# Stick-breaking attention: value products issued right ahead of the scores, and ScalarE's work in another order

## The reference

```
q, k, v, gate = split(h @ w_in, 4)          # q, k get an RMS norm per head
z = q . k / sqrt(64)                        # for keys before the query
log1m = -softplus(z)                        # 0 where masked
after = sum of log1m over the keys between this one and the query
wts = exp(log_sigmoid(z) + after)           # 0 where masked
o = wts @ v;   y = (o * silu(gate)) @ w_out
```

## Time and profile before

| what | value |
| --- | --- |
| median of 3 runs | 1758.52 us (1758.38 to 1759.03) |
| the profiled execution's own time | 1758.74 us |
| its span, first to last instruction | 1756.9 us |
| TensorE busy | 1741.8 us, 99% of the span |
| VectorE, ScalarE, GpSimd busy | 887.9, 826.3, 654.1 us |
| the attention layer's steps, first scores to last value products | 568.5 to 761.6 us of the span |

### The profile page before, as it was taken

The page is one execution under the profiler, slowest core; times in us unless marked ns, Lnnn a source line. Parts: engine busy times, 40 slices in busy tenths (PEclk is TensorE's granted clock), DMA queues, the critical chain, the costliest instruction groups (busy, mean ns, idle before and its releaser), DMA issues.

```text
span 1756.9 us, 22619 instructions
## 1 busy us (share of the span) xinstructions
PE 1741.8 (99%) x8786; PEld 1418.8 (81%) x8786; DVE 887.9 (51%) x1329; ACT 826.3 (47%) x1191; POOL 654.1 (37%) x238
## 2 busy tenths in 40 slices
PE   8999999999999999999999999999999999999999
PEld 6688899888898666678888888888877888998887
DVE  6765964453133777745734433341287568435500
ACT  5575343785233776744422222222266734348720
POOL 1333420344434655444244444444324234114442
PEclk9999999999999999999999999999999999999999
DMA  4223210222222111122222222222222232012222
GB/s 177 89 80 97 73 43 8 95 96 96 96 96 73 49 49 49 49 72 96 86 106 95 95 95 95 95 95 96 84 96 72 73 118 64 13 49 96 96 96 72
DMA packets 48776, 143.70 MB, mean 82 GB/s; under 512 B 28080, under 2 KB 30256, under 8 KB 32816
## 3 DMA queue, kind: packets, MB, share of 16 engines
q1 hardware_dynamic: 48688, 142.50, 23.9%
HBM read 137.25 MB, written 5.24 MB: 81 GB/s over the span
## 4 chain that ended last, share of the span: by engine, by line
PE 88%; DVE 6%; ACT 4%; issue 1%; DMA 0%; POOL 0%; SPq 0%; ACTq 0%; DVEq 0%
PE ps L1662 22%; PE ps L1664 22%; PE ps L1663 22%; PE ps L1928 3%; DVE acc L1154 2%; PE ps L1989 2%; PE ps L1955 2%; PE ps L2118 1%; PE ps L1975 1%; PE ps L1939 1%; PE ps L1984 1%; PE ps L2164 1%; DVE acc L1157 1%; PE ps L2062 1%; PE ps L2064 1%
## 5 line engine op out<-in xcount | busy, mean ns | idle before, releaser
L467 POOL TENSOR_TENSOR w_lo<-w_raw,w_hi 128x2048 fp32r<-128x2048 f32 x105 | 496.6, 4730 | 805.2 <-ACT w_hi L598 802.1
L1662 PE MATMUL ps<-h_hi,w_hi 128*128 128x512 f32 x1488 | 594.1, 399 | 4.2 <-DVE h_lo L1027 2.1
L1664 PE MATMUL ps<-h_hi,w_lo 128*128 128x512 f32 x1488 | 580.4, 390 | 0.0
L1663 PE MATMUL ps<-h_lo,w_hi 128*128 128x512 f32 x1488 | 579.5, 389 | 0.0
L1662 PEld LDWEIGHTS ps<-h_hi,w_hi 128*128 128x128 f32 x1488 | 279.4, 188 | 83.1 <-issue 21.1
L1664 PEld LDWEIGHTS ps<-h_hi,w_lo 128*128 128x128 f32 x1488 | 279.2, 188 | 59.8
L1663 PEld LDWEIGHTS ps<-h_lo,w_hi 128*128 128x128 f32 x1488 | 279.6, 188 | 55.9 <-issue 1.4
L598 ACT ACTIVATE w_hi<-w_raw 128x2048 fp32r<-128x2048 f32 (+1 forms) x126 | 238.7, 1895 | 129.4 <-PE ps L1664 123.8
L1662 PE MATMUL ps<-y_hi,w_hi 128*128 128x512 f32 x448 | 174.3, 389 | 0.0
L1663 PE MATMUL ps<-y_lo,w_hi 128*128 128x512 f32 x448 | 174.3, 389 | 0.0
L1664 PE MATMUL ps<-y_hi,w_lo 128*128 128x512 f32 x448 | 174.3, 389 | 0.0
(11 more groups left out here) (211 smaller groups left out, 2332.2 us busy)
## 6 DMA issues: line engine op xcount, KB each, us to landing
w_raw<-w_tiles SPq DMA_DIRECT2D x124, 1024.0 KB, 4.9
x<-x_t SPq DMA_DIRECT2D x4, 512.0 KB, 7.0
out_t<-x SPq DMA_DIRECT2D x8, 256.0 KB, 5.7
w_raw<-w_tiles SPq DMA_DIRECT2D x2, 512.0 KB, 5.0
scr_u<-lt SPq DMA_DIRECT2D x8, 128.0 KB, 2.7
u_blk<-scr_u SPq DMA_DIRECT2D x2, 512.0 KB, 3.3
scr_t<-v_t SPq DMA_DIRECT2D x2, 512.0 KB, 2.6
scr_v<-v_blk SPq DMA_DIRECT2D x2, 512.0 KB, 3.3
```

The costliest lines, as they stand in the source:

```text
L467: pool.tensor_tensor(w_lo[:, slot, :], w_raw[:, slot, :], w_hi[:, slot, :].bitcast(F32), ALU.subtract).then_inc(lo_done, 1)
L1662: pe.matmul(out_, w_h, m_h, start=start, stop=False)
L1663: pe.matmul(out_, w_h, m_l, start=False, stop=False)
L1664: return pe.matmul(out_, w_l, m_h, start=False, stop=stop)
```

## The change

Three orders are changed; no instruction is added, removed or resized.

- On TensorE, pv(g-2) goes from behind the blocks to the head of the step, right before z(g). The blocks that stood around it are now two before cum(g-1) and two after (in the last pair one and one).
- On ScalarE, in v = 2 and v = 3 weights(g-1) goes from behind softplus(g) to a place inside it, between Exp and Ln. In v = 0 and v = 1 it stays behind.
- On ScalarE, `hi` of tile t0 + 7 + j goes from the end of v = 2 in pair j to v = 0 of pair j + 1, behind softplus and before square_qk. The last one (pair 7, v = 3) stays.

```diff
@@ ScalarE, softplus(g, between)
                 for e in range(2):
                     act.wait_ge(b["abs"], 2 * g + e + 1)
                     act.activation(sb_t[:, e, 0:w], sb_t[:, e, 0:w], ACT.Exp, scale=-1.0).then_inc(b["exp"], 1)
+                if g % 4 > 1:
+                    weights(g - 1)
                 for e in range(2):
                     act.wait_ge(b["exp"], 2 * g + e + 1)
                     act.activation(sb_t[:, e, 0:w], sb_t[:, e, 0:w], ACT.Ln, bias=1.0).then_inc(b["ln1"], 1)
@@ ScalarE, the loop over pairs and steps
                     softplus(g, j + 1 if more and v == 3 else None)
+                    if v == 0 and j:
+                        hi(t0 + 6 + j)
                     if more and v == 0:
                         square_qk(j + 1, 0)
                     if more and v == 1:
                         rms_qk(j + 1, 0)
-                    if g:
+                    if g and v < 2:
                         weights(g - 1)
-                    if v == (2 if more else 3):
+                    if v == 3 and not more:
                         hi(t0 + 7 + j)
@@ TensorE, the loop over pairs and steps
                     g = 4 * j + v
+                    if g >= 2:
+                        pv(g - 2)
                     z(g)
                     if more and v == 3:
                         sums(j + 1, 1)
                     fill(2 if more else 1)
                     if more and v == 1:
                         sums(j + 1, 0)
-                    if g >= 2:
-                        pv(g - 2)
-                    fill(1 if more else 0)
                     if g:
                         cum(g - 1)
-                    fill(1)
+                    fill(2 if more else 1)
```

## The result

The changed kernel takes 1762.13 us (median of 13 runs, 1761.28 to 1763.62); the kernel before took 1758.96 us in the 13 runs beside it. The ratio is 1.0018 with a 95% interval of 1.001 to 1.0026: slower, by 3.2 us. The forecast was 1763.1 us, range 1757 to 1767.5, slower with a chance of 0.60. The profiled execution took 1762.0 us with a span of 1760.2.

What follows compares the result with a forecast made beforehand. TensorE, busy 99% of the span, was taken as the bound. Gains of 6.0 and 1.5 us against losses of 9.6 and 2.5 us gave +4.6 us on 1758.52: 1763.1 us, range 1757 to 1767.5.

Steps and rivals of the forecast that it cites:

- The join: TensorE, value products (pv) put right before scores (z): about 0.20 us saved per step, 30 places, 6.0 us.
- The chain on ScalarE: From z(v3)'s start: softplus sum at 5.90 us, z(v0) at 6.55, ScalarE's weights letting pv(v3) start at 13.27.
- The wait in v = 0: TensorE waits ahead of pv(v3) for ScalarE's weights: 1.6 us in each of six pairs, 9.6 us; last pair 2.5.
- my sum: TensorE's timeline from z(v3)'s start without the new wait: z(v0) at 6.55 us, ready for pv(v3) at 11.68.
- the last pair's other steps: Last pair outside v0: less time for ScalarE but an old wait gone; nothing was taken for these.
- Where the wait stands: The whole new wait, some 1.6 us per pair, was placed ahead of pv(v3), at the head of v = 1.
- TensorE stays the bound: Rival: weights(v3) ready by 11.68 us, so only gains count: 7.5 us less, 1751.0 us; chance 0.12.
- The old waits: TensorE's waits for ScalarE ahead of z(v0) and z(v1), 0.17 and 0.05 us, vanish: 0.22 x 7 = 1.5 us gained.
- a sign that it was wrong: The prediction said it would be wrong if, among other signs, a wait appeared at v2 or v3.
- the forecast's 0.3 us for the cast: VectorE's cast, starting while GpSimd's run_lo still runs, takes 0.73 us instead of 0.43, 0.3 us more.

Runs made afterwards that it cites:

- join alone: The kernel before with only TensorE's new order (pv(g-2) right before z(g)), ScalarE's order unchanged: 1761.41 us, ratio 1.0014.

## Why the prediction was right

The direction and the mechanism (hi queued ahead of the weights that pv(v3) waits for) were right, the place of the wait was right in part, and the time was inside the range. The net came out at 3.2 us instead of 4.6. By the steps:

- **The join**, 0.20 us at each of 30 places. Right. Without waits the steps are 6.08 (join alone), 4.97, 5.39 and 6.53 us, 22.97 in all; the pair before, less its waits of 0.22, was 23.85. That is 0.22 us per step, and the passage from pv to z costs what was assumed.
- **The chain on ScalarE.** From z(v3) at 655.81, the softplus sum of v = 3 starts at 5.92 (forecast 5.90), z(v0) at 6.53 (6.55), and pv(v3) at 13.11 (13.27). The difference of 0.16 lies mostly between the sum and v0's Ln, 3.35 instead of 3.46 us, where the cast was 0.63 us long and not 0.73.
- **The wait in v = 0**, forecast 1.6 us. z(v0) to z(v1) takes 7.39 to 7.86 us in the six pairs, 7.60 on the mean, against the 6.14 of my sum (11.68 - 6.55 + 1.01): 1.46 us, in all 8.8 instead of 9.6. In the last pair it is 7.06 against 4.74, 2.3 instead of 2.5. These two terms are 1.0 us too large together. The remaining 0.4 us are small things: the joins save a little more than 0.20 us each, and in the last pair's other steps new waits of 0.35 and 0.22 us stand against old ones of 0.17 and 0.55 that are gone. I had taken nothing for these without working them out; that they nearly cancel was luck.
- **Where the wait stands** was only partly right. In pair 4 some 0.6 us of it lie inside `cum`, 0.5 of them ahead of the second head (0.68 us from start to start where such a product takes 0.17), and 0.85 us ahead of pv(v3) (1.18 less 0.33), where I had put all of it. I had left VectorE's sp_lo out. In the changed kernel that made no difference, as one more block ahead of cum(v3) shows (1761.98 us); but I had not foreseen that this wait would lie inside the other, so the total owes something to luck.
- **The rival "TensorE stays the bound"** was stated wrongly. I let it decide from a ScalarE chain 1.6 us shorter. With hi's 1.8 us taken out of it the time was 1756, not 1751: VectorE's sums were the next limit, 0.6 us a pair, then square_qk ahead of the weights. With all three moved the time was 1753.5 us; square_qk and the weights exchanged without the later `cum` was not run.
- **The old waits** (0.22 us a pair) are gone, scaled_qk came down to 1.31 us (forecast about 1.1), and in the pairs j = 1 to 6 no wait showed in v = 2 or v = 3, as forecast. In the last pair there are two, the 0.35 and 0.22 us above, which the prediction had named as a sign that it was wrong; they are small beside the 11.1 us of v = 0.

## What to carry to other kernels

When work is moved to an engine that has idle time, ask which instruction is queued behind its new place and who waits for that one; with the same 1.8 us ahead of square_qk and the weights the kernel was 6.2 us slower than with them in the gap of v = 2. When an order on the bound engine is tightened, every input of every step is asked for sooner, not only the one that the edit names: list them all with the time at which each is there. Where a wait was taken away here, the next latest input took its place twice, so price the second limit before promising the first one's worth.

## What the runs showed of the hardware

GpSimd's sq_lo (L529) took 1.30 us before, where it started 1.1 us ahead of VectorE's low_w (665.96 and 667.10), and 2.80 us in the changed kernel. There it waits for square_qk, behind hi, and starts 0.6 us after low_w (the row names sb_sq, but that was done at 667.32, and square_qk at 667.90). First VectorE, then GpSimd:

```profile
667.41 2.29 DVE L1539 TENSOR_TENSOR w_lo<-w_raw,w_hi 128x2048 fp32r<-128x2048 f32 x1 [0.27 <-ACT w_hi L598]
```

```profile
668.03 2.80 POOL L529 TENSOR_TENSOR sq_lo<-sb_sq,sq_hi 128x512 fp32r<-128x512 f32 x1 [0.71 <-POOL sb_sq L524]
```

It ends 1.1 us after low_w does (670.83 against 669.70), close to its own length without company, as if it had not got on while low_w ran. The Trainium skill, SBUF — State Buffer, section SBUF: two separate sides, says just that: whoever starts first holds the pair of ports for the whole instruction. Here it was hidden, since TensorE asks for the sums later.

The traces speak for blocking rather than for a shared rate. In all twelve, sq_lo ends 1.12 to 1.17 us after low_w where it starts inside it, be it 0.26 or 0.97 us after low_w's start, and is 2.47 to 3.21 us long accordingly. The other way round, where low_w starts inside sq_lo, sq_lo keeps its 1.3 us and low_w ends some 2.15 us after it (2.27 where it starts only at sq_lo's end): with hi in the gap low_w once started 0.02 us behind sq_lo and took 3.41 us (594.29). Only two starts 0.01 us apart (hi back at the end of v = 2, 595.69 and 595.70) came out against the order of their rows. In the same way VectorE's cast to sp_hi (128x512), where it starts inside GpSimd's run_lo, ends 0.27 to 0.30 us after run_lo's end, whether it is then 0.45 us long or 1.60; the only ones that end later (0.35 to 0.37) start so late that they keep their own 0.43 us. The longest is in the last pair of the kernel before, VectorE first, then GpSimd:

```profile
751.15 1.60 DVE L1525 CAST sp_hi<-sb_sp 128x512 fp32r<-128x512 f32 x1
```

```profile
750.64 1.83 POOL L515 TENSOR_TENSOR run_lo<-run,run_hi 128x768 fp32r<-128x768 f32 x1
```

So the forecast's 0.3 us for the cast was not a fixed price: the cast pays for what is left of run_lo, and in the changed kernel that made it 0.2 us.
